# Decode attention over a paged cache: keys transposed by VectorE in 32x32 blocks, scores as 32-row products in sixteen array tiles, in place of TensorE transposes

## The chip, the cores and the metric

The kernel runs on one core of one Trainium2 chip. The metric is the device time in microseconds (us) of one launch; smaller is better. Three timed executions of the kernel before are given, and one profiled execution, whose trace all rows below come from.

## What is computed

One inference step of a two-layer decoder trunk for 512 prompt tokens and 8 decode rows (one new token in each). Layer 0 is a state-space layer, layer 1 multi-head latent attention with 16 heads; each layer stands between two SwiGLU blocks. The change touches only the latent attention of the 8 decode rows over their 2048 cached positions:

```python
def latent_attention(q_lat, q_pe, q_pos, key_sets):
    for c, kpe, k_pos in key_sets:       # c (b,k,256), kpe (b,k,32)
        s = einsum('bqhr,bkr->bhqk', q_lat, c) + einsum('bqhe,bke->bhqk', q_pe, kpe)
        scores.append(where(k_pos <= q_pos, s * scale, NEG_BIG))
    p = softmax(concatenate(scores, -1), -1)
    return sum(einsum('bhqk,bkr->bqhr', p_part, c))
...
c_past = cache_ckv[page_table].reshape(b_s, 2048, 256)
kpe_past = cache_kpe[page_table].reshape(b_s, 2048, 32)
```

So for each decode row b: 16 pages of 128 positions, each page 128x256 latents and 128x32 rotary keys, 16 heads. Everything is float32.

## The kernel before

One program, an instruction stream for each engine written out by hand, with semaphores between them; no scheduler reorders anything. The big matrix products of the trunk (feed-forward, projections) fill most of the time; then come the attention of the prompt (eight pairs of heads, `for i in range(NH // 2)`, scores, softmax, transposed probabilities, weighted values), and behind it the decode rows, `for b in range(NB)`, and the output projection (`wo_half`, `product`), which begins inside the last decode row.

**The decode rows.** The pages of row b land in `cb[b % 3]` (latents, positions on partitions) and `kb[b % 3]` (rotary keys). `page_loader` issues them, SP (SyncE) pages 0 to 8 and POOL (GpSimd) pages 9 to 15, in the order pages 0, keys 0, pages 1, keys 1, keys 2, pages 2, keys 3, pages 3, keys 4 and so on; `pages(b)` waits until the row three before has been read by its last product (`d_o`), `pages(2)` until the prompt attention's last output is in place (`a_ol`). Behind `caches()` SP loads `uv` and the columns of the output projection.

A score needs the latent dimension on partitions, so the keys of a row are transposed on TensorE (PE): `turned(b, q)`, q = 0 to 8, four 128x128 transposes each into one PSUM bank (three banks in turn), 32 of latents and 4 of rotary keys. ScalarE (ACT) copies the even q to SBUF, VectorE (DVE) the odd ones, into `cbT` (and `kbT`). The scores of a row are then 8 products 128 rows x 32 columns x 512 positions with `qlat` and 16 of 128 positions with `qpe`, four at a time in the four column strips of the array, into one bank: partition 32c + h holds head h and the positions of pages 4c to 4c+3. DVE takes the maximum (L2291, L2292), ACT the exponential (L1532), PE transposes the probabilities (4 transposes), DVE copies them to SBUF as `pbT` (L2301), and PE makes the 16 weighted products with `cb` (L3258), which ACT copies to `ob` (L1537).

PE's order in iteration b of `for b in range(NB)`: scores of b, the turns 0 to 3 of row b+1, the transposes of the probabilities, turns 4 to 8 of row b+1, weighted products of b. So the turns fill the time of the softmax. The turns of row 0 stand between the last steps of the prompt attention. Row 7 has `wo_half` in their place.

```python
src = cb[j][:, 4 * (q % 4) + s, (q // 4) * P:(q // 4) * P + P]          # PE, turned
got = turn(ps[:, (0, 1, 7)[n % 3], s * P:s * P + P], src)
...
mm(ps[HP * c:HP * c + HP, 2 + j, :], qlat[:, r, b, :], cbT[:, r, KB * c:KB * c + KB], ...)   # PE, scores
```

Of the kernel before, what the change touches and what calls it, by code (L numbers as in the profile page):

```python
# [19 lines left out]
F32 = mybir.dt.float32  # L20
# [3 lines left out]
ALU = mybir.AluOpType  # L24
# [3 lines left out]
P = 128  # L28
# [42 lines left out]
KB = PAST // NQ  # L71
NEG = -1e30
# [184 lines left out]
def yoco_step(nc, inp, out):  # L257
# [6 lines left out]
    with ctx:  # L264
# [57 lines left out]
        with ExitStack() as s:  # L322
# [16 lines left out]
            with ExitStack() as m:  # L339
# [3 lines left out]
                    m, ("cbT", [P, RT, PAST], F32), ("cb2", [P, NPG, R], F32), ("mb", [P, NB], F32), ("nmb", [P, NB], F32),  # L343
# [82 lines left out]
        def pair_of(dst, s):  # L426
# [9 lines left out]
        kbT = tb[:, 0, 0:4 * P].rearrange("p (g k) -> p g k", g=4)  # L436
# [34 lines left out]
        d_uv, d_pt, d_t, d_ta, d_td, d_s, d_m, d_e, d_pt2, d_pe, d_o, d_oe, d_rt, d_w, d_we, d_ws, d_wp, d_l, d_fin, d_of, d_oh, d_ol = (  # L471
            sem("dec_" + n) for n in ("uv", "pt", "tr", "tr_a", "tr_d", "s", "max", "exp", "p_tr", "p_sb", "o", "o_sb", "rows",
                                      "logw", "w", "w_norm", "w_ps", "lat_ps", "fin", "of", "oh", "ol"))
        d_le = sem("dec_lat_rows")
# [146 lines left out]
        def page_loader(eng, arrived, ckv, kpe):  # L621
# [351 lines left out]
        def _(act):  # L973
# [508 lines left out]
            def turned(b, q):  # L1482

                act.wait_ge(d_t, b * 9 + q + 1)
                if b >= 1:
                    act.wait_ge(d_s, b)
                src = ps[:, (0, 1, 7)[(b * 9 + q) % 3], :]
                if q < 8:
                    run(cbT[:, q // 4, (q % 4) * 512:(q % 4) * 512 + 512], src, ACT.Copy).then_inc(d_ta, 1)
                else:  # L1490
                    run(kbT[:, :, :], src.rearrange("p (g k) -> p g k", g=4), ACT.Copy).then_inc(d_ta, 1)

            for i in range(NH // 2):
# [13 lines left out]
                if more:  # L1507
                    softmax(i + 1, 2)
                    softmax(i + 1, 3)
                else:  # L1510
                    turned(0, 0)
                probs(i, 4)
            turned(0, 2)
            turned(0, 4)
            weighted(NH // 2 - 1)
            turned(0, 6)
            turned(0, 8)


            for b in range(NB):  # L1520
                if b + 1 < NB:
                    turned(b + 1, 0)
                else:
# [8 lines left out]
                run(pb, ps[:, 2 + b % 2, :], ACT.Exp, bias=nmb[:, b:b + 1], scale=SCALE, accum_out=lb[:, b:b + 1]).then_inc(d_e, 1)  # L1532
                if b + 1 < NB:
# [3 lines left out]
                run(ob[:, b, :], ps[:, 5 + b % 2, 0:R], ACT.Copy).then_inc(d_oe, 1)  # L1537
# [1954 lines left out]
```

## Time and profile before

| | us |
|---|---|
| three timed executions | 2007.0, 2008.1 (median), 2010.79 |
| profiled execution, span from first to last instruction | 2007.1 |
| PE (matmul records) busy | 1960.4 (98% of the span) |
| PE weight loads busy | 1875.2 (93%) |
| DVE, ACT, POOL busy | 1277.0, 820.4, 132.8 |
| decode rows, from the first score to the last (1507.77 to 1578.34) | 70.6 |

The profile gives no total of its own for the profiled execution beside its span, which lies 1.0 us below the median of the timed ones. One float32 product is recorded as two weight loads and two matmuls (passes), one transpose as one of each, so a count behind an x is twice the number of float32 products. A bracket behind a row is the time that the engine was idle before it and what it waited for. "PEclk" is the granted TensorE clock as a share of 2.4 GHz.

### The profile page before, as it was taken

How to read it: one execution, taken by the hardware profiler on the slowest of the kernel's cores; microseconds unless marked ns; L12 is line 12 of the kernel's file. 1: busy time of each engine (PE TensorE's matmuls, PEld its weight loads, DVE VectorE, ACT ScalarE, POOL GpSimd, SP SyncE). 2: the span in 40 equal slices, each digit the busy share in tenths (PEclk: the TensorE clock that was granted, in tenths of full speed). 3: DMA queues.
4: the chain of work that ended last, by engine and by line, in shares of the span. 5: the costliest groups of instructions: out<-in, count | busy, mean ns of one | idle time of the engine just before them, and what ended most of it. 6: DMA issues, size and time to landing. Idle time of an engine off the chain costs nothing.

```text
span 2007.1 us, 41612 instructions
## 1 busy us (share of the span) xinstructions
PE 1960.4 (98%) x17604; PEld 1875.2 (93%) x17604; DVE 1277.0 (64%) x1771; ACT 820.4 (41%) x1243; POOL 132.8 (7%) x231
## 2 busy tenths in 40 slices
PE   8999999988999999999999999999989999999999
PEld 7999999987999999999999999997666799999998
DVE  6445486697469577576884856655764349668474
ACT  5332233343245244255452534454654244345252
POOL 3002002010000000000000000000047000000000
PEclk9999999989999999999999999999999999999999
DMA  7233234864342322234322322231248422323222
GB/s 151 84 102 88 75 93 115 269 140 100 95 137 85 120 89 95 77 105 116 97 85 85 127 85 86 84 101 51 54 119 231 149 71 83 127 85 120 91 74 75
DMA packets 260624, 211.55 MB, mean 105 GB/s; under 512 B 42372, under 2 KB 235426, under 8 KB 260450
## 3 DMA queue, kind: packets, MB, share of 16 engines
q1 hardware_dynamic: 248528, 187.52, 31.9%
q0 software_dynamic: 6656, 13.69, 2.4%
q10 hardware_dynamic: 5266, 7.85, 1.2%
q8 instruction: 130, 2.13, 0.4%
q14 instruction: 44, 0.36, 0.1%
HBM read 195.29 MB, written 10.33 MB: 102 GB/s over the span
## 4 chain that ended last, share of the span: by engine, by line
PE 67%; DVE 3%; ACT 2%; issue 2%; SPq 1%; DMA 1%; DVEq 0%; ACTq 0%
PE ps L2459 25%; PE ps L2487 25%; PE ps L2388 6%; PE ps L2401 2%; PE ps L2947 1%; PE ps L3053 1%; PE ps L3209 1%; PE ps L3086 1%; SPq L654 1%; SPq L639 1%; DMA cb<-cache_ckv 1%; PE ps L2841 1%; PE ps L3030 1%; DVE wl L1668 0%; DVE xl L1619 0%
## 5 line engine op out<-in xcount | busy, mean ns | idle before, releaser
L2388 PE MATMUL ps<-xh,wh 128*128 128x260 f32 x1088 | 286.9, 285 | 2.6 <-DVE xl L1619 1.4
L2388 PE MATMUL ps<-xl,wh 128*128 128x260 f32 x1088 | 283.7, 283 | 0.0
L2487 PE MATMUL ps<-xoh,wh 128*128 128x260 f32 x992 | 281.3, 284 | 1.3 <-DVE sq L1835 1.3
L2487 PE MATMUL ps<-xoh,wl 128*128 128x260 f32 x992 | 281.0, 283 | 0.0
L2487 PE MATMUL ps<-xol,wh 128*128 128x260 f32 x992 | 280.6, 283 | 0.0
L2459 PE MATMUL ps<-xh,wh 128*128 128x260 f32 x872 | 228.8, 284 | 0.6 <-DVE wl L1668 0.6
L1067 ACT ACTIVATE wh<-rw 128x1024 fp32r<-128x1024 f32 (+1 forms) x135 | 138.8, 1029 | 218.6 <-PE ps L2459 151.7
L2459 PE MATMUL ps<-xl,wh 128*128 128x260 f32 x872 | 227.0, 282 | 0.0
L2388 PE MATMUL ps<-xh,wl 128*128 128x260 f32 x1088 | 219.3, 283 | 0.0
L990 ACT ACTIVATE wh<-raw 128x1024 fp32r<-128x1024 f32 (+1 forms) x90 | 100.4, 1116 | 283.4 <-PE ps L2388 250.5
L2388 PEld LDWEIGHTS ps<-xh,wh 128*128 128x128 f32 x1088 | 205.6, 189 | 6.9 <-issue 3.9
L2388 PEld LDWEIGHTS ps<-xl,wh 128*128 128x128 f32 x1088 | 205.1, 188 | 0.0
L1668 DVE TENSOR_TENSOR wl<-rw,wh 128x1024 fp32r<-128x1024 f32 (+1 forms) x135 | 160.3, 1188 | 67.3 <-ACT wh L1067 67.2
L2487 PE MATMUL ps<-xoh,third 128*128 128x260 f32 x1040 | 198.6, 283 | 0.6 <-DVE sq L1835 0.6
L2487 PEld LDWEIGHTS ps<-xoh,wh 128*128 128x128 f32 x992 | 186.6, 188 | 1.6 <-DVE wl L1668 1.6
L2487 PEld LDWEIGHTS ps<-xol,wh 128*128 128x128 f32 x992 | 186.9, 188 | 0.0
L2487 PEld LDWEIGHTS ps<-xoh,wl 128*128 128x128 f32 x992 | 186.8, 188 | 0.0
L1579 DVE TENSOR_TENSOR wl<-raw,wh 128x1024 fp32r<-128x1024 f32 (+1 forms) x92 | 120.5, 1310 | 89.5 <-ACT wh L990 81.8
L2459 PE MATMUL ps<-xh,wl 128*128 128x260 f32 x872 | 175.5, 283 | 0.0
L2388 PEld LDWEIGHTS ps<-xh,wl 128*128 128x128 f32 x1088 | 167.9, 189 | 0.0
L2459 PEld LDWEIGHTS ps<-xh,wh 128*128 128x128 f32 x872 | 164.4, 189 | 1.7 <-DVE wl L1668 1.1
L2487 PEld LDWEIGHTS ps<-xoh,third 128*128 128x128 f32 x1040 | 164.8, 188 | 0.8 <-DVE third L1668 0.8
(550 smaller groups left out, 4202.2 us busy)
## 6 DMA issues: line engine op xcount, KB each, us to landing
rw<-ffn_w_gate SPq DMA_DIRECT2D x33, 1024.0 KB, 5.4
rw<-ffn_w_up SPq DMA_DIRECT2D x33, 1024.0 KB, 8.0
rw<-ffn_w_down SPq DMA_DIRECT2D x12, 2048.0 KB, 7.8
raw<-ffn_w_gate SPq DMA_DIRECT2D x22, 512.0 KB, 3.9
raw<-ffn_w_up SPq DMA_DIRECT2D x22, 512.0 KB, 3.9
raw<-ffn_w_down SPq DMA_DIRECT2D x16, 704.0 KB, 4.8
rw<-ffn_w_down SPq DMA_DIRECT2D x6, 1536.0 KB, 6.7
cb<-cache_ckv SPq DMA_DIRECT2D x72, 128.0 KB, 3.7
```

The source lines that it names most:

```text
L639: eng.dma_start(kb[j][:, g, :], inp["cache_kpe"][bass.ds(numbers[b][g], 1)].rearrange("a p r -> p (a r)")).then_inc(arrived[j], 16)
L654: eng.dma_start(cb[j][:, g, :], inp["cache_ckv"][bass.ds(numbers[b][g], 1)].rearrange("a p r -> p (a r)")).then_inc(arrived[j], 16)
L990: run(wh[par_][:, 0:size], raw[par_][:, 0:size], ACT.Copy).then_inc(w_hi, 1)
L1067: run(as_slot(name, slot_h(name, n), n), raw_of(name, n), ACT.Copy).then_inc(z_hi, 1)
L1579: tt(wl[par_][:, 0:size], raw[par_][:, 0:size], wh[par_][:, 0:size], ALU.subtract).then_inc(w_lo, 1)
L1668: tt(as_slot(name, slot_l(name, n), n), raw_of(name, n), as_slot(name, slot_h(name, n), n), ALU.subtract).then_inc(z_lo, 1)
L2388: got = mm(ps[0:width, bank + half, 0:HALF], w[par_][:, k * width:k * width + width], src[:, k0 + k, half * HALF:half * HALF + HALF], star ...
L2401: return nc.tensor.transpose(dst, src, ident[0:rows, 0:rows])
L2459: got = mm(ps[:, bank + half, T0], w[:, cols], src_[:, k, half * HALF:half * HALF + HALF], start=first and m == 0 and s == 0, stop=last an ...
L2487: got = mm(ps[:, bank + mat, T0], w[:, cols], src[:, j, k, :], start=first and k == 0 and m == 0 and s == 0, stop=k == 3 and m == 1, skip_ ...
L2841: got = mm(ps[:, bank + half, 0:HALF], w[slot][:, k * P:k * P + P], src[:, k, half * HALF:half * HALF + HALF], start=k == 0 and m == 0 and ...
L2947: got = mm(ps[:, 2 * (i % 2) + half, 0:HALF], cols, src[:, k, half * HALF:half * HALF + HALF], start=k == 0 and o == 0 and s == 0, stop=k ...
```

## The change

1. **Keys.** `turned` goes from PE, ACT and DVE to DVE alone: five `V.transpose` instructions a row, each of which transposes every 32x32 block where it stands, SBUF to SBUF: q = 0 the rotary keys (128x512), q = 1 to 4 a quarter of the latents each (64 of 256 columns of all 16 pages, 128x1024). Partition group g (32 partitions) of `cbT` then holds latent dimension within a block of 32, for the positions 32g to 32g+31 of each page.
2. **Scores.** A product now contracts over 32 rows only: `cache_scores(b, q)`. For each of 8 blocks of 32 latent dimensions, and once for the rotary keys, 16 products of 32 rows x 16 heads (32 columns for the rotary keys) x 128 positions, one for each of the four row groups g and four column strips c: 144 products a row in place of 24. Row group g adds up in bank `SC_BANK + g`, so the scores of a row take four banks, 128 columns each, and there is one set of them.
3. **Queries.** Since each row group multiplies all 256 latent dimensions, `qlat` is copied to all four partition groups (`qrep`, in the columns of `cst` that held the cosines): 16 DMAs of 32 partitions x 256 elements on POOL's queue, ahead of its `caches()`.
4. **Softmax.** DVE's maximum and ACT's exponential read the four banks; ACT instead of DVE copies the transposed probabilities.
5. **Waits.** The exponential of row b must have read the banks before the scores of row b+1 begin. `keys(b)` waits for turn 0 of the row three before, not for all nine turns.

```diff
@@ the scores' views, page_loader
-        kbT = tb[:, 0, 0:4 * P].rearrange("p (g k) -> p g k", g=4)
+        kbT = tb[:, 0, 0:NPG * DR].rearrange("p (g e) -> p g e", g=NPG)
+        qrep = cst[:, C_COS:C_COS + NRB * NB * NH].rearrange("p (q r b h) -> p q r b h", q=NQ, r=RT, b=NB)
+        sc = ps[:, SC_BANK:SC_BANK + NQ, 0:P]
...
-                    eng.wait_ge(d_t, 9 * (b - 2))
+                    eng.wait_ge(d_t, TURNS * (b - 3) + 1)
@@ ACT, for b in range(NB)
-                run(pb, ps[:, 2 + b % 2, :], ACT.Exp, bias=nmb[:, b:b + 1], scale=SCALE, accum_out=lb[:, b:b + 1]).then_inc(d_e, 1)
-                if b + 1 < NB:
-                    for q in range(2, 9, 2):
-                        turned(b + 1, q)
+                run(pb.rearrange("p (s g t) -> p g s t", s=NQ, g=NQ), sc.rearrange("p g (s t) -> p g s t", s=NQ), ACT.Exp,
+                    bias=nmb[:, b:b + 1], scale=SCALE, accum_out=lb[:, b:b + 1]).then_inc(d_e, 1)
+                act.wait_ge(d_pt2, b + 1)
+                if b >= 1:
+                    act.wait_ge(d_o, b)
+                run(pbT[:, :, :], ps[:, PT_BANK, :].rearrange("p (m q) -> p m q", m=NQ), ACT.Copy).then_inc(d_pe, 1)
@@ DVE, turned(b, q)
-                dve.wait_ge(d_t, b * 9 + q + 1)
-                if b >= 1:
+                j = b % 3
+                if q == 0:
+                    dve.wait_ge(d_in[j], (b // 3 + 1) * 16 * N_SP)
+                    dve.wait_ge(d_kin[j], (b // 3 + 1) * 16 * N_POOL)
+                    if b == 0:
+                        dve.wait_ge(a_s, NH // 2 * NSS)
+                if b >= 1 and q < NTP:
+                    dve.wait_ge(d_sp, NTP * (b - 1) + q + 1)
+                elif b >= 1:
                     dve.wait_ge(d_s, b)
-                copy(cbT[:, q // 4, (q % 4) * 512:(q % 4) * 512 + 512], ps[:, (0, 1, 7)[(b * 9 + q) % 3], :]).then_inc(d_td, 1)
+                if q == 0:
+                    V.transpose(kbT, kb[j][:, :, :]).then_inc(d_t, 1)
+                else:
+                    cols = slice(RG * TURN_W * (q - 1), RG * TURN_W * q)
+                    V.transpose(cbT[:, :, cols], cb[j][:, :, cols]).then_inc(d_t, 1)
@@ DVE, for b in range(NB)
+                if b + 1 < NB:
+                    turned(b + 1, 0)
                 dve.wait_ge(d_s, b + 1)
-                own(V.tensor_reduce(mb[:, b:b + 1], ps[:, 2 + b % 2, :], AX.X, ALU.max))
+                own(V.tensor_reduce(mb[:, b:b + 1], sc, AX.XY, ALU.max))
                 ts(nmb[:, b:b + 1], mb[:, b:b + 1], -SCALE, None, ALU.mult).then_inc(d_m, 1)
                 if b + 1 < NB:
-                    turned(b + 1, 1)
-                    turned(b + 1, 3)
+                    for q in range(1, TURNS):
+                        turned(b + 1, q)
@@ PE
+            def cache_scores(b, q):
+
+                pe.wait_ge(d_t, TURNS * b + q + 1)
+                if q == 0 and b == 0:
+                    pe.wait_ge(d_qr, 16 * NQ * NQ)
+                    pe.wait_ge(a_ol, NH // 2)
+                elif q == 0:
+                    pe.wait_ge(d_e, b)
+                for k in range(TURN_W * (q - 1), TURN_W * q) if q else (NRB,):
+                    for g in range(NQ):
+                        rows = slice(RG * g, RG * (g + 1))
+                        for c in range(NQ):
+                            pages_ = slice(NQ * c, NQ * (c + 1))
+                            if k < NRB:
+                                heads, w, src = NH, qrep[rows, k % NQ, k // NQ, b, :], cbT[rows, pages_, RG * k:RG * (k + 1)]
+                            else:
+                                heads, w, src = HP, qpe[rows, b, g, :], kbT[rows, pages_, :]
+                            got = mm(ps[HP * c:HP * c + heads, SC_BANK + g, 0:P], w, src, start=q == 0, stop=k == NRB - 1, skip_group_check=True)
+                got.then_inc(d_sp if q < NTP else d_s, 1)
...
                 for m in range(NQ):
-                    got = turn(ps[:, 4, m * P:m * P + P], pb[:, m * P:m * P + P])
+                    got = turn(ps[:, PT_BANK, m * P:m * P + P], pb[:, m * P:m * P + P])
                 got.then_inc(d_pt2, 1)
                 if b + 1 < NB:
-                    for q in range(4, 9):
-                        turned(b + 1, q)
+                    cache_scores(b + 1, 0)
...
+                weighted_rows(b)
+                if b + 1 < NB:
+                    for q in range(1, TURNS):
+                        cache_scores(b + 1, q)
@@ POOL, ahead of caches()
+            pool.wait_ge(l_qe, 1)
+            for g in range(NQ):
+                for k in range(NQ):
+                    pool.dma_start(qrep[RG * g:RG * (g + 1), k, :, :, :], qlat[RG * k:RG * (k + 1), :, :, 0:NH]).then_inc(d_qr, 16)
```

**PE, from the last transposes of the prompt attention's probabilities (`pp`) to the weighted products of row 0.** First before, then now. `cb` and `kb` are transposed keys, `pT,vv` the last pair's values, `ta` the probabilities of the decode rows; an x counts instructions.

```order
L2401 MATMUL ps<-cst,pp 128x128 x3
L2401 MATMUL ps<-cst,cb 128x128 x16
L3086 MATMUL ps<-pT,vv 64x512 x2
...
L2401 MATMUL ps<-cst,kb 128x128 x4
L3223 MATMUL ps<-cbT,qlat 32x512 x8
L3227 MATMUL ps<-tb,qpe 32x128 x16
L2401 MATMUL ps<-cst,cb 128x128 x16
L2401 MATMUL ps<-cst,ta 128x128 x4
L2401 MATMUL ps<-cst,cb 128x128 x16
L2401 MATMUL ps<-cst,kb 128x128 x4
L3258 MATMUL ps<-cb,ta 32x256 x16
```

```order
L2398 MATMUL ps<-cst,pp 128x128 x20
L3083 MATMUL ps<-pT,vv 64x512 x2
...
L3203 MATMUL ps<-tb,qpe 32x128 x16
L3203 MATMUL ps<-cbT,cst 16x128 x128
L2398 MATMUL ps<-cst,ta 128x128 x4
L3203 MATMUL ps<-tb,qpe 32x128 x16
L3213 MATMUL ps<-cb,ta 32x256 x16
```

No key transposes are left on PE: between the probabilities' transposes and the weighted products stand only the 16 rotary products of the next row, and its 128 latent products follow behind.

**DVE, the loop over decode rows, from the weighted output (`xl`) of the prompt's last pair through row 1's maximum.** First before, then now; `tb` holds the transposed rotary keys, `mb` and `nmb` the maximum, `ta` the copied probabilities.

```order
L2235 TENSOR_TENSOR xl<-ps,xh 128x512
L2247 COPY cbT<-ps 128x512
L2291 TENSOR_REDUCE mb<-ps 128x1
L2292 TENSOR_SCALAR nmb<-mb 128x1
L2247 COPY cbT<-ps 128x512 x2
L2301 COPY ta<-ps 128x512
L2247 COPY cbT<-ps 128x512 x2
L2291 TENSOR_REDUCE mb<-ps 128x1
```

```order
L2226 TENSOR_TENSOR xl<-ps,xh 128x512
L2249 STREAM_TRANSPOSE cbT<-cb 128x16x64 x3
L2246 STREAM_TRANSPOSE tb<-kb 128x512
L2295 TENSOR_REDUCE mb<-ps 128x1
L2296 TENSOR_SCALAR nmb<-mb 128x1
L2249 STREAM_TRANSPOSE cbT<-cb 128x16x64 x4
L2246 STREAM_TRANSPOSE tb<-be 128x512
L2295 TENSOR_REDUCE mb<-ps 128x1
```

The rotary transpose of the next row, which waits until that row's pages have landed, now stands ahead of the maximum of the present row.

## Rows read from the trace of the kernel before

**Rows 1.** The page's head.

```profile
span 2007.1 us, 41612 instructions
```

**Rows 2.** Timeline of PE in the decode rows: start, us, instruction, [idle before].

```profile
1529.80 2.00 PE L2401 MATMUL ps<-cst,cb 128*128 128x128 f32 x16 [0.49 <-DMA cb<-cache_ckv]
1531.81 0.66 PE L2401 MATMUL ps<-cst,ta 128*128 128x128 f32 x4
1532.30 1.94 PE L2401 MATMUL ps<-cst,cb 128*128 128x128 f32 x16
...
1534.71 1.93 PE L3258 MATMUL ps<-cb,ta 128*32 128x256 f32 x32
1536.46 1.90 PE L3223 MATMUL ps<-cbT,qlat 128*32 128x512 f32 x16
...
1539.16 2.00 PE L2401 MATMUL ps<-cst,cb 128*128 128x128 f32 x16
...
1568.97 2.00 PE L2401 MATMUL ps<-cst,cb 128*128 128x128 f32 x16 [0.95 <-DMA cb<-cache_ckv]
...
1578.34 0.39 PE L3209 MATMUL ps<-xh,wh 128*128 128x260 f32 x1
```

**Rows 3.** Timeline of SP's queue: when it issues the pages and keys.

```profile
1507.16 4.45 SPq L654 DMA_DIRECT2D cb<-cache_ckv  x9
...
1553.88 4.56 SPq L639 DMA_DIRECT2D kb<-cache_kpe  x8
1558.62 4.83 SPq L654 DMA_DIRECT2D cb<-cache_ckv  x9
```

**Rows 4.** Windows: us, busy PE, PEld, DVE, ACT, POOL, PEclk, DMA share, GB/s.

```profile
1507.77:1578.34 70.57, 68.41 (x889) 47.87 (x889) 30.86 (x51) 29.39 (x58) 43.98 (x82) 1.00 0.79 229
```

**Rows 5.** Groups of DVE by form in the whole span: busy, mean ns, idle before.

```profile
L1680 DVE TENSOR_TENSOR be<-rw 128x1024 f32<-128x1024 f32 x15 | 18.3, 1218 | 0.0
...
L2086 DVE TENSOR_TENSOR x<-x,tb 128x512 f32<-128x512 f32 x8 | 8.9, 1114 | 0.0
...
L2291 DVE TENSOR_REDUCE mb<-ps 128x1 f32<-128x512 f32 x8 | 5.5, 691 | 32.4 <-PE ps L3227 32.4
...
L2292 DVE TENSOR_SCALAR nmb<-mb 128x1 f32<-128x1 f32 x8 | 1.2, 154 | 0.3
```

**Rows 6.** Timeline of PE in the state-space layer: products in fewer and smaller tiles.

```profile
443.72 1.89 PE L2853 MATMUL ps<-sn,ct 128*32 128x8 f32 x128 [0.81 <-ACT last_in L1302]
...
470.30 1.97 PE L2804 MATMUL ps<-tsh,ush 128*64 128x128 f32 x32 [0.18 <-ACT yr L1313]
472.19 1.98 PE L2817 MATMUL ps<-ctcw,xsr 64*64 64x128 f32 x64
```

**Rows 7.** Groups of ACT by form in the decode rows, 1507 to 1580.

```profile
L1489 ACT ACTIVATE cbT<-ps 128x512 f32<-128x512 f32 x28 | 16.7, 597 | 29.1 <-PE ps L2401 29.1
L1532 ACT ACTIVATE ta<-ps,nmb 128x512 f32<-128x512 f32 x8 | 5.5, 682 | 1.2 <-DVE nmb L2292 1.2
...
L1532 ACT ACTIVATION_READ_ACCUMULATOR ta<-ps,nmb 128x1 f32 x8 | 1.6, 200 | 0.0
```

**Rows 8.** Timeline of PE at the end of the prompt attention.

```profile
1501.37 1.94 PE L2401 MATMUL ps<-cst,cb 128*128 128x128 f32 x16
1503.25 2.37 PE L3086 MATMUL ps<-pT,vv 128*64 128x512 f32 x16
```

**Rows 9.** Windows, columns as in rows 4: PE idle, then the granted clock.

```profile
475.20:477.00 1.80, 0.00 (x0) 0.00 (x0) 1.73 (x5) 1.80 (x4) 0.00 (x0) 1.00 0.00 0
477.05:478.96 1.91, 1.91 (x65) 1.74 (x65) 1.87 (x2) 0.32 (x1) 1.64 (x4) 1.00 0.00 0
...
1484.70:1488.00 3.30, 1.46 (x12) 1.02 (x10) 3.06 (x7) 1.48 (x5) 2.83 (x6) 1.00 1.05 311
1488.10:1491.40 3.30, 3.15 (x15) 2.69 (x16) 1.27 (x5) 1.41 (x5) 3.14 (x7) 0.50 0.66 91
```

**Rows 10.** Timeline of POOL: its first decode pages.

```profile
1466.20 4.05 POOL L654 DMA_DIRECT2D cb<-cache_ckv  x7 [150.32 <-DMA qs<-qq]
```

More of the change, by code:

```diff
@@ L71 @@
 KB = PAST // NQ
+RG = P // NQ
+NRB = R // RG
+TURN_W = 2
+NTP = NRB // TURN_W
+TURNS = NTP + 1
+SC_BANK, PT_BANK = 4, 3
 NEG = -1e30
@@ L2269, in _ @@
                 else:
-                    turned(0, 1)
+                    turned(0, 0)
                 probs(i, 5)
@@ L2277, in _ @@
                     normalise(i + 1, 3)
-            turned(0, 3)
-            turned(0, 5)
+            turned(0, 1)
             weighted(NH // 2 - 1)
-            turned(0, 7)
+            for q in range(2, TURNS):
+                turned(0, q)
             def wide_lo(j):
@@ L3185, in _ @@
                 turned_probs(i, 3)
-                if not more:
-                    turned(0, 0)
                 turned_probs(i, 4)
-                if not more:
-                    turned(0, 1)
                 turned_probs(i, 5)
@@ L3193, in _ @@
                     values(i // 2 + 1, i % 2)
-            for q in range(2, 6):
-                turned(0, q)
             weighted(NH // 2 - 1)
-            for q in range(6, 9):
-                turned(0, q)
             def wo_half(d, half, k0, k1):
@@ new lines, in weighted_rows @@
+            def weighted_rows(b):
+                pe.wait_ge(d_pe, b + 1)
+                if b >= 2:
+                    pe.wait_ge(d_oe, b - 1)
+                for m in range(NQ):
+                    for c in range(NQ):
+                        got = mm(ps[HP * c:HP * c + HP, 1 + b % 2, 0:R], pbT[:, m, HP * c:HP * c + HP], cb[b % 3][:, 4 * c + m, :],
+                                 start=m == 0, stop=m == NQ - 1, skip_group_check=True)
+                got.then_inc(d_o, 1)
+            for q in range(TURNS):
+                cache_scores(0, q)
@@ L3234, in _ @@
+            for b in range(NB):
                 if b == NB - 1:
-                    pe.wait_ge(a_ol, NH // 2)
                     wo_half(0, 0, 0, KD)
@@ L3248, in _ @@
                     turn(ps[0:NB, 7, P:2 * P], lb[:, :]).then_inc(d_rt, 1)
+                    pe.wait_ge(d_oe, NB - 1)
                     wo_half(1, 0, 0, 3)
-                pe.wait_ge(d_pe, b + 1)
-                if b >= 2:
-                    pe.wait_ge(d_oe, b - 1)
-                elif b == 1:
-                    pe.wait_ge(a_ol, NH // 2)
-                for m in range(NQ):
-                    for c in range(NQ):
-                        got = mm(ps[HP * c:HP * c + HP, 5 + j, 0:R], pbT[:, m, HP * c:HP * c + HP], cb[b % 3][:, 4 * c + m, :],
-                                 start=m == 0, stop=m == NQ - 1, skip_group_check=True)
-                got.then_inc(d_o, 1)
+                weighted_rows(b)
+                if b + 1 < NB:
+                    for q in range(1, TURNS):
+                        cache_scores(b + 1, q)
             wo_half(1, 0, 3, KD)
+            pe.wait_ge(d_oe, NB)
             wo_half(2, 0, 0, 3)
```

68 lines of the change are left out of this document (6 added, 62 removed).

## The prediction

> **What bounds the kernel now.** Look at the windows first. In the 70.6 us of the decode rows PE is busy for 68.4, at a granted clock of 1.00 (2.4 GHz), DVE for 30.9 and ACT for 29.4 [rows 4]. PE looks like the bound, and the timeline of PE says what a decode row costs it, by the starts of the rows: 1529.80 to 1539.16 is 9.36 us, of which 1.75 are the weighted products (1534.71 to 1536.46), 0.49 the transposes of the probabilities (1531.81 to 1532.30), 2.70 the scores (1536.46 to 1539.16), and the rest, 4.42, the transposes of the keys [rows 2]. The same timeline shows a second bound close behind: PE waits for a page DMA at 1529.80 and again at 1568.97, in front of rows 3 and 7. These two are four rows apart, 39.17 us, so pages arrive every 9.79 us, just slower than PE's 9.36. SP's queue says why. Eight issues of keys and nine of pages follow each other without a wait: keys at 1553.88, pages at 1558.62, done at 1563.45, so 9.57 us for one row's issues [rows 3]. The last pages land 10.35 us after SP began to issue them (1558.62 to 1568.97), and 9.37 us later the last score is done and `wo_half` begins at 1578.34 [rows 2, 3].
>
> So the change has to be read against the page traffic. It takes work from PE, but the pages set the pace of rows 3 to 7, and the change moves none of their DMAs. What it can win is the start of the chain and what lies behind the last landing.
>
> **PE's part.** Removed: 4.42 us of transposes a row and 2.70 of scores. Added: 144 products, 288 records by the trace's count. What one costs is the question. The nearest rows: 64 records of 64x64 tiles (four tiles, two row groups) with 128 columns take 1.98 us, 30.9 ns each, while 32 records of 128x64 tiles with the same columns take 1.97, 61.6 ns each [rows 6]. Halving the rows of a tile halved the time of a record: row groups do run beside each other. Sixteen tiles are four times as many as four, so I take 30.9/4 = 7.7 ns: 288 x 7.7 = 2.2 us a row. The bounds: at the cheap end nothing below that, since the columns must stream; at the dear end 30.9 ns (four tiles at once only), 8.9 us a row. Between them lies the row of 128 records with 8 columns, 1.89 us, 14.8 ns each [rows 6], which carries weight loads of twice the columns and mostly no streaming, so issue alone costs at most that.
>
> The Trainium skill has a rule that speaks against the change: in "TensorE: Matmul & The Clock Gate", section "Wait — 56ns, not 53.3ns?", start-to-start never drops below about 25 ns, however small the product. By that rule the change loses; it is the first rival below. The trace does not bear it out: 14.8 ns is already less.
>
> **DVE's part.** Removed: four copies and the copy of the probabilities a row. Added: one transpose of 512 elements and four of 1024 a partition. No row shows a DVE transpose. The nearest is an SBUF to SBUF operation of 128x1024 float32, 1.22 us [rows 5]; at the same rate 512 take some 0.69, as the reduction of 512 does. I take these: 0.69 + 4 x 1.22 = 5.6 us, plus 0.69 for the maximum and 0.15 for the scaling, 6.4 a row with nothing waiting. The dear end is the strided addition of 512 elements at 1.11 us, 2.2 ns an element: 2.2 us for 1024, 10 for a row's transposes [rows 5].
>
> **ACT's part.** It loses five copies and gains the copy of the probabilities, 0.60, after its exponential of 0.68 and 0.20 for the sum [rows 7]; half its load is gone, so it costs nothing but its place in the chain.
>
> **The cycle.** With one set of score banks PE can't score ahead any more. From the last score of a row: maximum and scaling 0.84, exponential and sum 0.88, transposes of the probabilities 0.49, weighted products 1.75, and four handovers and their latencies, which I put at 0.7 (an estimate): 4.7 us, plus 288 records. At 7.7 ns the copy of the probabilities isn't covered by the 32 rotary records and adds about 0.4: 7.3 us. DVE's own cycle is 6.4 and some 0.4 of handovers. Both are below 9.79, so the pages stay the bound. The cycle meets 9.79 at (9.79 - 4.7)/288 = 17.7 ns a record. Below that PE's price hardly counts, above it every ns costs 0.29 us a row.
>
> **The order of DVE.** Turn 0 of row b+1 stands ahead of the maximum of row b and waits for row b+1's pages. So row b's softmax is held until those have landed, and with it `d_o`, which frees the buffer for row b+3: landing, about 5.9 us to the end of the weighted products (the first six terms below, with their handovers), then 10.35 to land again, 16.3 for two rows, 8.1 a row. Below 9.79, so it doesn't slow the queue. But it moves row 6's softmax behind the last landing: from there, rotary turn 0.69, maximum 0.84, exponential 0.88, transposes 0.49, copy 0.60, weighted 1.75, the 256 latent records 2.0 and handovers 0.5: 7.7 us (DVE's side, 0.69 + 0.84 + 4.9 + 0.6, is 7.0). Before it was 9.37. Gain 1.7.
>
> **The start.** PE loses 16 transposes between the last probabilities and the last weighted product, 1501.37 to 1503.25 [rows 8]; DVE gets the rotary turn of 0.69 ahead of the copy that product waits for. I take 1.0 of the 1.9 as won; `a_ol` and with it SP's pages of row 2 (1507.16) come that much sooner, and the whole chain of pages with them. The query copies lie in the 150 us in which POOL waits for nothing else [rows 10]: hidden, and if the cover were gone, 16 of POOL's issues at 0.58 (4.05/7 by the same row), 9 us, would stand ahead of the pages.
>
> **The clock.** PE will be idle for about 5 us of every 9.8, where before it had no gap over a microsecond. An idle stretch may cost it the full clock: in 1484.70 to 1488.00 it was busy for 1.46 of 3.30, and the next 3.30 us ran at 0.50 (1.2 GHz); after 1.80 us of idleness at 475.20 it ran on at 1.00 [rows 9]. At half clock the last chain grows by 0.5 + 1.75 + up to 1.8 = 4.0 us. I charge 0.7: which of the products fall into a slow stretch is open, and a part of the loss hides under DVE's side of the tail, which has 0.7 us to spare.
>
> **Sum** against the profiled span, 2007.1 [rows 1]: -1.0 - 1.7 + 0.7 = -2.0, so 2005.1; on the median, 1.0 above it, 2006.1 us. Runs of this kernel scatter by about 0.2%, 4 us, so this would read as no change.
>
> **Rivals.**
> *Products cost more than 17.7 ns* (ends slower). For: 31 ns in four tiles, and no row has sixteen; against: the halving from 61.6 to 30.9, and 14.8 ns. At 25 ns the cycle is 4.7 + 7.2 = 11.9, and row 0's scores end 7.2 us after 1506.2: 1513.4 + 7 x 11.9 = 1596.7, 18.4 later than 1578.34: 2026.5. At 30.9: 13.6 a cycle, 1515.1 + 95.2 = 1610.3: 2040. The rule of the skill would give the first of these. Chance 0.18.
> *DVE transposes at the strided price.* DVE's cycle is 1.1 + 4 x 2.25 + 0.84 + 0.4 = 11.3: 1506.2 + 3 x 2.25 + 0.6 + 7 x 11.3 = 1592.7, +14.3: 2022.4. Against: the blocks read runs of 64 elements. Chance 0.10.
> *The clock falls in every row.* The tail's 4.0 instead of 0.7, and as much of `wo_half` at half clock: +1.3 to +4 in all, 2009.4 to 2012. At 14.8 ns a record some 2 more. Chance 0.12.
> *The pages come faster.* An undisturbed issue of SP takes 4.45/9 = 0.49 us [rows 3], 17 of them and the gaps between the groups 8.8; if PE's lighter load lets the queue run at that pace, five rows win 0.8 each on top of 2.7: 2001. Against: both queues and the DMA engines see the same traffic. Chance 0.10.
> *Row groups take turns*, so that the change doesn't do what it says: 27 to 31 ns, part of the first rival.
> The forecast has 0.50.
>
> **How the numbers follow.** Slower by over 0.2%: the first two rivals, 0.28, half of the third's worst, 0.04, and 0.02 of the forecast: 0.34. Faster: most of the fourth, 0.09, and 0.06 of the forecast, whose start may win the whole 1.9. Within: 0.51. The range goes from 2001.0 to 2024.0: it takes in DVE's rival and the clock's, and leaves out the dear products.
>
> **What would show it.** PE's timeline: groups of 128 `cbT` products, some 1 us for 128 records; above 2.3 (17.7 ns) the first rival holds. DVE's groups: transposes of 128x1024 at 1.22. PE waiting for DVE's turn 0 and that for the DMA, rows 9.8 us apart. PEclk in the windows of 1510 to 1580. If the rows come at under 9 us apart, or the last score is later than 1580, I am wrong.

## The result, and the profile after

| | before | changed |
|---|---|---|
| four timed executions each, median (lowest to highest), us | 2007.95 (2007.0 to 2010.79) | 2036.15 (2035.85 to 2036.27) |
| ratio, 95% interval | | 1.0124 (1.0106 to 1.0143) |
| span of the profiled execution, us | 2007.1 | 2034.3 |
| last decode score done, us | 1578.34 | 1604.10 |

The change costs 28 us, and 26 of them are there when the last score is done. The forecast of 2006.1 was wrong, and its range, up to 2024, did not hold the time. This is the timeline of PE in the changed kernel over two rows, with the columns of [rows 2]; L3203 is `cache_scores` (`tb`: rotary, `cbT`: latent), L3213 `weighted_rows`, L2398 `turn`.

```profile
1527.42 0.65 PE L2398 MATMUL ps<-cst,ta 128*128 128x128 f32 x4 [1.79 <-ACT ta L1521]
1528.37 0.51 PE L3203 MATMUL ps<-tb,qpe 32*32 32x128 f32 x32 [0.29 <-issue]
1528.81 1.94 PE L3213 MATMUL ps<-cb,ta 128*32 128x256 f32 x32
1530.68 1.04 PE L3203 MATMUL ps<-cbT,cst 32*16 32x128 f32 x64
1532.94 1.85 PE L3203 MATMUL ps<-cbT,cst 32*16 32x128 f32 x128 [1.23 <-issue]
1537.24 1.47 PE L3203 MATMUL ps<-cbT,cst 32*16 32x128 f32 x64 [2.46 <-issue]
1540.50 1.11 PE L2398 MATMUL ps<-cst,ta 128*128 128x128 f32 x4 [1.78 <-ACT ta L1521]
1541.54 0.73 PE L3203 MATMUL ps<-tb,qpe 32*32 32x128 f32 x32
1542.30 3.64 PE L3213 MATMUL ps<-cb,ta 128*32 128x256 f32 x32
1545.87 3.69 PE L3203 MATMUL ps<-cbT,cst 32*16 32x128 f32 x250
1551.85 0.40 PE L3203 MATMUL ps<-cbT,cst 32*16 32x128 f32 x6 [2.29 <-issue]
1554.04 1.11 PE L2398 MATMUL ps<-cst,ta 128*128 128x128 f32 x4 [1.79 <-ACT ta L1521]
```

The two rows start 13.08 and 13.54 us apart, where before it was 9.36 and the pages' pace 9.79 [rows 2]. (Over six rows, from 1516.43 to 1592.66, the mean is 12.7.) The second one, read against the forecast's cycle of 7.3 us, term by term: the transposes of the probabilities take 1.04 instead of 0.49, the rotary products 0.76 where 0.25 was charged for them (32 records at 7.7 ns) and 0.4 for the copy that outlasts them, the weighted products 3.57 instead of 1.75, the latent products 3.69 and 0.40 instead of 2.0, an idle stretch of 2.29 that no term had, and 1.79 of waiting for the exponential, which holds the 1.72 forecast for maximum, exponential and sum.

The windows, with the columns of [rows 4], say why some of these are twice what they should be (PEclk is the last column but two): the whole stretch of decode rows; the stretch of 10.2 us in which the clock stayed down; and 128 latent records at full clock.

```profile
1508.00:1604.00 96.00, 67.32 (x2556) 40.87 (x2556) 46.22 (x55) 14.21 (x30) 44.13 (x82) 0.77 0.59 170
```

```profile
1536.46:1546.66 10.20, 7.61 (x176) 3.81 (x185) 5.97 (x7) 1.76 (x4) 3.81 (x8) 0.50 0.56 158
```

```profile
1532.94:1534.79 1.85, 1.85 (x128) 1.41 (x128) 0.18 (x1) 0.00 (x0) 1.67 (x5) 1.00 0.92 218
```

The mean granted clock of the decode rows fell from 1.00 [rows 4] to 0.77: the transposes, rotary and weighted products of most rows run at 0.50 (1.2 GHz). The latent products are dear for another reason: 128 records take 1.85 us, 14.5 ns each, at the full clock.

What was idle, from the waits of 1508 to 1604 (who waited for whom, us in total, times, longest):

```profile
ACT ta L1521 <- DVE nmb L2296: 47.2, 7, 8.5
DVE mb L2295 <- PE ps L3203: 41.4, 7, 7.5
...
PE ps L3203 <- issue: 15.3, 9, 2.5
POOL cb L662 <- PE ps L3213: 15.2, 3, 5.8
...
PE ps L2398 <- ACT ta L1521: 12.6, 7, 1.8
...
DVE tb L2246 <- DMA cb<-cache_ckv: 0.4, 1, 0.4
```

DVE waits for PE's scores and practically never for pages (0.4 us), while POOL waits for PE before it may load the next row. The bound has moved from the pages to PE, which is itself idle: 12.6 us for the exponentials and 15.3 us for nothing that the profile shows. DVE is as forecast, in its groups (columns as in [rows 5]):

```profile
L2249 DVE STREAM_TRANSPOSE cbT<-cb 128x1024 f32<-128x1024 f32 x32 | 37.0, 1212 | 0.0
L2295 DVE TENSOR_REDUCE mb<-ps 128x1 f32<-128x512 f32 x8 | 5.5, 692 | 49.4 <-PE ps L3203 49.4
```

The idle stretches have a companion in the DMA queues of 1508 to 1604 (packets, MB, share of 16 engines). This is the changed kernel:

```profile
q8 instruction: 19, 0.31, 1.4%
```

And the kernel before, in the same stretch:

```profile
q8 instruction: 9, 0.15, 0.6%
```

A packet has 16 KB (0.31 MB / 19). Each record of PE stands for a weight load and a matmul, so 128 records are 256 instructions, and if a packet holds those it has 64 bytes for each. The Trainium skill, "Perfetto Trace Analysis", section "The 4-stage abstract model", calls instructions 64-byte ones, which gives the same. Theory SUPPLY: these packets are PE's own instruction stream, and PE runs dry when short products use up a block faster than the next one comes.

The totals of whole executions bear out whose packets they are. The kernel before, with 17604 records of PE, the changed kernel, with 19236, and the kernel of experiment 10 with three row groups, with 20796, read:

```profile
q8 instruction: 130, 2.13, 0.4%
```

```profile
q8 instruction: 143, 2.34, 0.5%
```

```profile
q8 instruction: 155, 2.54, 0.5%
```

1632 records more are 12.75 blocks of 128, and 13 packets more; 1560 more are 12.2 blocks, and 12 packets.

### The profile page after: what moved, and what is told of

Read it like the earlier page. It is cut to its first block, busy times and chain, and to the rows that moved or that the text cites. A ratio compares the mean times of both kernels' runs of the same rounds, so it can differ in the third digit from the quotient of the medians.

```text
span 2034.3 us, 44797 instructions
## 1 busy us (share of the span) xinstructions
PE 1963.4 (97%) x19236; PEld 1870.8 (92%) x19236; DVE 1291.5 (63%) x1771; ACT 803.1 (39%) x1211; POOL 143.1 (7%) x247
## 4 chain that ended last, share of the span: by engine, by line
PE 68%; DVE 4%; issue 3%; ACT 2%; DVEq 0%; ACTq 0%
PE ps L2456 25%; PE ps L2484 24%; PE ps L2385 6%; PE ps L3203 2%; PE ps L2398 2%; PE ps L3213 1%; PE ps L2944 1%; PE ps L3050 1%; PE ps L3181 1%; PE ps L3083 1%; PE ps L3027 1%; PE ps L2838 1%; DVE wl L1659 0%; DVE xl L1610 0%; DVE mx L2201 0%
```

## The experiments

Times of all but the two bursts are medians of at least four executions, each ratio against the kernel before on the same chip. On those chips the executions scattered by up to 13 us, so a difference of a few us between two of them is not a finding; the profiles carry the argument.

**1. Keep the clock up: wide products in the gap.**

```diff
+            def filler(b, n):
+                if b < NB - 1:
+                    for _ in range(n):
+                        mm(ps[:, 0, :], ident, cb[b % 3][:, 0:2, :].rearrange("p g r -> p (g r)"), start=True, stop=True, ...)
...
+            filler(0, 2)
...
                     for q in range(1, TURNS):
                         cache_scores(b + 1, q)
+                    filler(b + 1, 2)
```

> Added: behind the last score of rows 0 to 6 TensorE issues two float32 products 128x128 by 512 columns into a bank that nothing reads (an estimate of 0.9 to 1.8 us, in the 1.8 us in which it waits for the exponential). Theory CLOCK (the rows are long because TensorE runs at 1.2 GHz in their first half): the granted clock in 1508 to 1604 rises from about .75 to over .9, the weighted products of a row take 1.94 us instead of 3.64 and the row pace falls from 12.8 to about 11: 2036 - 7 x 1.8 = 2023 us. Theory SUPPLY (TensorE's instruction stream is fetched in blocks and runs dry once or twice a row under the dense short products): the idle stretches put down to issue (15.3 us, 9 times in 96 us) stay, so no more is won than the clock's part, and what the faster clock wins is partly taken by longer stretches of that kind: 2026 to 2034. Theory RECORDS (a product simply costs 14 ns a record at any clock): no change of the latent products' time, 2028.

Measured: 2035.28 us, ratio 1.0124 (1.0091 to 1.0157). The timeline of PE over one row and a half:

```profile
1544.04 1.06 PE L2398 MATMUL ps<-cst,ta 128*128 128x128 f32 x4
1545.03 0.51 PE L3203 MATMUL ps<-tb,qpe 32*32 32x128 f32 x32
1545.79 1.93 PE L3219 MATMUL ps<-cb,ta 128*32 128x256 f32 x32 [0.25 <-ACT ta L1526]
1547.65 1.70 PE L3203 MATMUL ps<-cbT,cst 32*16 32x128 f32 x110
1549.69 1.87 PE L3203 MATMUL ps<-cbT,cst 32*16 32x128 f32 x128 [0.34 <-issue]
1553.44 0.45 PE L3203 MATMUL ps<-cbT,cst 32*16 32x128 f32 x18 [1.88 <-issue]
1553.81 1.98 PE L3210 MATMUL ps<-cb,cst 128*128 128x512 f32 x4
```

The weighted products are at 1.93 us in every row, and the time did not move. It lies above what any of the three theories gave: the stretches of issue grew to 17.7 us (L3203 and L3210 together), among them one of 4.61, and the filler itself took 2 to 3.8 us. So the half clock alone does not explain the loss. The rows are 13.05 us apart in the mean (1518.33 to 1596.61, six rows). They show two more things. Where two stretches follow each other within a row's scores, exactly 128 records lie between them, as in the changed kernel at 1532.94. And a stretch that in the changed kernel stood behind record 250 of its row stands here behind record 110 + 128 = 238, 12 earlier. By then three fillers of four records each have been added. The same holds row by row: 201 (0 added), 192 against 184 (8), 250 against 238 (12), 181 against 165 (16), 239 against 219 (20), 170 against 146 (24) and 228 against 200 (28). PE stops at fixed places of its instruction stream, whatever it waits for in the program.

**2. One wide product instead of two** (`filler(b + 1, 1)`).

> One wide product behind the last score of rows 0 to 6 instead of two; at full clock the two took 1.98 us, so one takes 1.0, inside the 1.79 us of waiting. Theory CLOCK ADDS (half clock costs a row 2.4 us: 1.7 in the weighted products, 0.45 and 0.23 in the transposes and rotary products): if one product keeps the clock, 2036 - 7 x 2.4 = 2019; the earlier run with two showed the full clock and lost as much in front of the transposes. Theory NOT ENOUGH: one product does not keep the clock in most rows, weighted products of 3.6 us stay and the time with them: 2034 to 2038. Theory SUPPLY says that the stretches of issue stay in either case (12 to 16 us in 1508 to 1604), their places in the stream two records a row earlier than in the changed kernel.

Measured: 2028.95 us, ratio 1.0094 (1.0057 to 1.013). Mean clock 0.86 instead of 0.77, weighted products 385 ns in the mean instead of 548, rows 11.9 us apart (1517.31 to 1576.89, five rows). The stretches of issue grew to 19.2 us, 11 times. One of 4.37 us, 1583.09 to 1587.46, lies beside the large loads of the output projection, in a window with the DMA share at 1.08. So the time came down by some 7 us of the 28, which the intervals of the two ratios, overlapping as they do, leave uncertain by several; the theory that only the clock costs time had asked for 17. The clock was won in a part only, and the longer stretches are time that came back as waiting for instructions. The clock also changes the price of the latent products, which the changed kernel's rows show less clearly: 98 records from 1587.46 took 2.04 us at 0.50, 20.8 ns each, and 125 from 1524.04 2.61 us, 20.9 ns.

**3. Fewer products.** Half, then three quarters of the latent blocks:

```diff
-                for k in range(TURN_W * (q - 1), TURN_W * q) if q else (NRB,):
+                for k in ((q - 1) * TURN_W,) if q else (NRB,):
```

> Left out: every second block of latent scores, so 80 products (160 records) a row instead of 144 (288); VectorE's transposes all stay. Theory SUPPLY: 128 instructions and their weight loads less a row, the stretches of issue fall from 15.3 us to under 5, the row pace from 12.8 to about 9.8 to 10.5 where the pages bound it again: about 2008 to 2014 us. Theory RECORDS: 128 records x 14 ns = 1.8 us a row off, 12.8 to 11.0: 2024 us, the stretches of issue as before. Theory CLOCK: TensorE does less, so the clock stays low or falls further; 2024 or later.

> Left out: two of the eight blocks of latent scores, so 112 products (224 records) a row. Theory SUPPLY (a block of the stream is 128 records; 261 records a row instead of 325): one stretch of issue less in three rows besides the 0.95 us of the records themselves, stretches 5 to 9 us in all, total 2018 to 2024. Theory RECORDS: 64 x 14.8 ns = 0.95 us a row, 7.6 in all: 2028.

Measured: half, 2011.11 us, ratio 1.0003 (0.9992 to 1.0014); three quarters, 2020.5, ratio 1.0054 (1.0034 to 1.0073). With half the blocks, the waits of 1508 to 1581 read:

```profile
DVE tb L2246 <- DMA cb<-cache_ckv: 22.2, 6, 5.1
...
PE ps L3203 <- issue: 2.2, 1, 2.2
```

Now DVE waits for pages in front of six rows, as the forecast had it for the whole change, and the only stretch of issue is 2.2 us. The weighted products still take 3.5 to 3.6 us in five of seven rows: the half clock is there and costs the rows little, since the pages pace them (experiment 4 tests that). By the record (14.5 ns) the missing products are worth 64 x 14.5 = 0.93 us a row for each quarter, 7.4 us in all. The first quarter won some 15 us (15.7 by the medians, 14 by the ratios), and its stretches of issue fell from 15.3 us to 10.3 (5 to 9 were expected; the time lies in the expected 2018 to 2024).

**4. Half of the blocks and one wide product** (the edits of 2 and 3 together).

> Left out: every second block of latent scores (80 products a row); added: one wide product behind the last score of rows 0 to 6. Without the addition this kernel took as long as the kernel before, with the weighted products at 3.6 us in six of seven rows and VectorE waiting 22 us for pages. Theory PAGES BOUND IT: the full clock shortens work that is hidden behind the pages, 2008 to 2011, with weighted products at 1.94 us if the product keeps the clock. Theory CLOCK: the half clock is still on the path, 2.4 us a row off: 1995 to 2003.

Measured: 2011.75 us, ratio 1.0009 (0.9999 to 1.0019), weighted products at 505 ns in the mean instead of the 548 of experiment 3, and DVE waiting 23.4 us for pages. The clock was won in three of seven rows (1.93 us for the weighted products), and behind those rows PE waited some 5 us for the exponential, which the next pages held up, where behind the others it waited some 1. So it did not move the time: with few instructions the pages are the bound.

**5. Less page traffic.**

```diff
+                rows = slice(0, P if b < 3 else 16)
                 for g in ckv:
-                    eng.dma_start(cb[j][:, g, :], ...)
+                    eng.dma_start(cb[j][rows, g, :], ...[rows])
```

> Left out: for rows 3 to 7 only 16 of 128 positions of each latent page are loaded (an eighth of the page traffic, the same number of DMAs). Theory SUPPLY with contention (the instruction blocks of 16 KB are late because the pages hold the DMA engines): the stretches of issue vanish in the rows whose time no longer has page traffic, the row pace falls to about 11 there: 2036 - 5 x 2 = 2026. Theory SUPPLY by density alone: the blocks take as long, stretches and time stay: 2034 to 2037. Theory CLOCK or RECORDS: no change, 2034 to 2037. Theory PAGES (the traffic is the bound as forecast): 2015 or less.

Measured: 2032.98 us (2025.54 to 2034.48), ratio 1.0114 (1.0091 to 1.0138). The stretches stand behind the same records (250, 181, 239, 170, 228), from 1.27 to 1.96 us long in place of 1.56 to 2.29. Together they are 7.7 us in place of 9.6; three are shorter, one is the same and one longer (1.96 in place of 1.56). So the traffic may lengthen them, and it is not what makes them; most of the loss is there without it: the time lies between the 2026 expected of contention and the 2034 to 2037 of density alone, nearer to the latter. The profiled execution is the fastest of the four, the one of 2025.54 us.

**6. The order of DVE:** `turned(b + 1, 0)` behind the maximum.

> VectorE takes turn 0 of row b+1 (the rotary keys, 0.69 us) behind the maximum of row b instead of ahead of it, so the softmax of row b no longer waits for the pages of row b+1. My forecast charged that order with nothing because the pages set the pace; since the pages do not bound the rows now, turn 0 is done long before the last score and every theory expects no change: 2035 to 2037. If the row b+1 pages still held the softmax, up to 0.7 us a row would be won: 2031.

Measured: 2033.89 us, ratio 1.0113 (1.0084 to 1.0143). No change, as expected.

**7. Another order on PE:** long products among the short ones.

```diff
-                weighted_rows(b)
...
+                    cache_scores(b + 1, 1)
+                    weighted_rows(b, 0, 2)
+                    cache_scores(b + 1, 2)
+                    weighted_rows(b, 2, NQ)
+                    cache_scores(b + 1, 3)
+                    cache_scores(b + 1, 4)
```

> The same instructions in another order on TensorE: scores 1 of row b+1 ahead of the weighted products of b, scores 2 between their halves, scores 3 and 4 behind. Theory SUPPLY: the stretches of issue come from blocks of 128 short records in a row; with 32 long records (60 to 114 ns each) spread among them the block lasts longer than its fetch and the stretches fall from 15 us to some 8: 2028, and the copy of the probabilities is covered. Theory DENSITY OVER A ROW (325 records a row are too many in any order): 2034 to 2038. Theory RECORDS or CLOCK: 2034 to 2038, since neither changes; a change of the tile form costs something, up to 0.2 us a row.

Measured: 2036.54 us, ratio 1.0126 (1.0101 to 1.0151). The stretches fell to 10.7 us, and the rows did not come faster (1540.67, 1553.75, 1567.58), most of them with the weighted products at half clock still (514 ns in the mean). The 2028 of theory SUPPLY was missed: shorter stretches did not bring shorter rows. I don't have every us of this run; it shows that spreading the short products did not pay.

**8. Another order of the tiles:** by diagonals, `c = (g + o) % NQ`.

> The sixteen products of a block in another order: each differs from the one before in row group and column strip (by the diagonal), where the changed kernel runs four strips of one row group. Theory ISSUE (14.8 ns is the rate at which TensorE takes a weight load and a matmul, whatever tile they go to): 128 records stay at 1.85 to 1.88 us, 2034 to 2038. Theory TILES (row groups run beside each other, strips of one row group do not): 128 records fall towards 1.0 us, 1.7 us a row less, and the stretches of issue grow by a part of that: 2024 to 2032.

Measured: 2033.68 us, ratio 1.013 (1.0097 to 1.0163). 128 records take 1.85 us as before: between these two orders the price does not depend on which tile follows which.

**9. Short products in the kernel before,** 64 a row, of one row group, ahead of its scores:

```diff
+                for n in range(64):
+                    c = n % NQ
+                    mm(ps[HP * c:HP * c + HP, 2 + j, 0:P], qlat[0:HP, n // NQ % RT, b, :], cbT[0:HP, 0, P * c:P * c + P], ...)
```

> The kernel before, with 64 products (128 records) of 32x32 tiles with 128 columns ahead of the scores of each row, whose result the scores overwrite. TensorE's 9.36 us a row become 11.3, above the pages' 9.79, so 8 rows cost at least 8 x 1.9 - 3 = 12 us: 2019 to 2022 if 128 short records are worth 1.9 us and no more (theory RECORDS). Theory SUPPLY: 270 records a row in all, of which half are long, so a block of 128 lasts 4 us on the mean; stretches of issue in some rows only, 0 to 6 us more: 2020 to 2027. That the stretches occur in the old order of work too, where VectorE does no transposes, would show that they do not belong to the change's waits.

Measured: 2050.01 us, ratio 1.019 (1.0158 to 1.0222), far more than either theory gave. The timeline of PE over a row:

```profile
1539.21 1.93 PE L3262 MATMUL ps<-cb,ta 128*32 128x256 f32 x32
1541.07 3.70 PE L3223 MATMUL ps<-cbT,qlat 32*32 32x128 f32 x128
1544.70 3.62 PE L3227 MATMUL ps<-cbT,qlat 128*32 128x512 f32 x16
1548.08 1.11 PE L3231 MATMUL ps<-tb,qpe 128*32 128x128 f32 x32
```

Windows of the two middle groups:

```profile
1541.07:1544.77 3.70, 3.70 (x136) 3.50 (x136) 0.00 (x0) 0.38 (x1) 2.73 (x6) 1.00 0.63 186
1544.77:1548.00 3.23, 3.23 (x16) 0.74 (x20) 0.00 (x0) 0.00 (x0) 2.99 (x6) 0.50 0.97 306
```

On one row group 128 records take 3.70 us at the full clock, 28.9 ns each, twice the price on four. And behind them the clock is at 0.50, the scores 3.62 us instead of 1.92, although PE had no idle stretch at all from 1520 to 1620. So it is in five of the seven rows of this stretch; in the other two (1555.90 and 1600.25) the scores behind the short products take 1.92. So short products on 32-row tiles can be followed by the half clock where nothing waits. The rows come 14.8 us apart (1524.68 to 1613.38, six rows) in place of 9.36: 3.6 of the 5.4 are the added products, and the rest is mostly the half clock, which neither theory had charged. There are no stretches of issue here, against what SUPPLY had expected for some rows: 128 records in 3.70 us are about as slow as the pieces of experiment 10 (3.5 to 3.75 us), and long products follow them.

**10. Bursts** in the changed kernel, two executions each: behind row 2 and row 6, 256 products on two row groups; then, behind six wide ones, 384 on three.

```diff
...
+                for i in range(n):
+                    g, c = i // NQ % 3, i % NQ
+                    rows, bank = slice(RG * g, RG * (g + 1)), (0, 3, 1 + b % 2)[g]
+                    mm(ps[HP * c:HP * c + NH, bank, 0:P], qrep[rows, c, 0, b, :], cb[b % 3][rows, c, 0:P], ...)
...
+                        filler(b + 1, 6)
+                        burst(b + 1, 384)
```

> Added: 256 products (512 records) of 32x16 tiles with 128 columns, back to back and waiting for nothing, behind the last score of row 2 (page traffic beside them) and of row 6 (the large weight loads beside them), into banks that nothing reads. Theory SUPPLY: each burst breaks up into pieces of 128 records of 1.9 us with stretches of issue between them, 1.3 us or more each and longer where the DMA engines are busy: 11 to 18 us a burst, 2058 to 2072 us in all. Theory WAITS (the stretches belong to something that the scores of a row wait for, the transposes or the banks): the bursts run through, 7.6 us each: 2051.

> Added behind the last score of rows 2 and 6: six wide products (128x128 by 512 columns, about 6 us at full clock), then 384 products (768 records) of 32x16 tiles on three row groups in turn. The question is how fast blocks of 128 short records can come at all. In the runs so far a block of 1.9 us was followed by 1.88 us of idleness where nothing else disturbed it, 3.75 us a block; the burst on two row groups ran at half clock with 3.77 us a block and without gaps, so it could not tell the array's pace from the supply's. Three row groups need at most 2.5 us a block (29.4 x 2/3 = 19.6 ns a record at half clock), 1.9 at full clock. Theory SUPPLY WITH A FLOOR: pieces of 128 records, 3.75 us from start to start at either place, longer under page traffic: bursts of 22 us or more. Theory CONTENTION ONLY: with the DMA engines idle (behind row 6's large loads) the pieces follow each other without a gap, 11 to 15 us a burst. On the clock: after six wide products it is 1.00, and it falls to 0.50 within the burst although TensorE never stops, if short tiles are what lets it fall; theory IDLENESS (only waiting lets it fall) says 1.00 throughout.

Measured: 2063.69 and 2084.35 us. On two row groups each burst has one gap at a block's end (3.01 and 3.28 us) and then runs without one at half clock, 448 records in 13.19 us, 29.4 ns each; the time lies in the range of theory SUPPLY, but the pieces that it expected did not appear, so this burst decides nothing. On three, the timeline of PE behind row 6:

```profile
1618.87 3.74 PE L3218 MATMUL ps<-cb,cst 32*16 32x128 f32 x274
1624.78 2.93 PE L3218 MATMUL ps<-cb,cst 32*16 32x128 f32 x128 [2.16 <-issue]
1628.53 2.93 PE L3218 MATMUL ps<-cb,cst 32*16 32x128 f32 x128 [0.83 <-issue]
1632.29 2.93 PE L3218 MATMUL ps<-cb,cst 32*16 32x128 f32 x128 [0.83 <-issue]
1636.05 2.57 PE L3218 MATMUL ps<-cb,cst 32*16 32x128 f32 x110 [0.83 <-issue]
```

And its windows:

```profile
1618.87:1622.61 3.74, 3.74 (x275) 3.31 (x274) 0.00 (x0) 0.00 (x0) 0.00 (x0) 1.00 0.02 4
1624.78:1638.55 13.77, 11.28 (x495) 8.57 (x495) 0.00 (x0) 0.00 (x0) 0.00 (x0) 0.50 0.02 5
```

These products wait for nothing, the DMA share is 0.02, and still a piece of 128 begins every 3.75 us (1624.78, 1628.53, 1632.29, 1636.05). Behind row 2 the same: 1547.17, 1550.92, 1554.68, then 3.48 and 3.47. The first 180 and 274 records run through, at 13.7 to 14.2 ns; I read this as what had been fetched while PE did long work. With it the bursts took 20.1 and 19.7 us, between the 22 or more of a floor from the first record and the 11 to 15 of contention alone. In the second burst, 1618.87 to 1638.55, five instruction packets moved, about one for each piece. That speaks for SUPPLY with a floor and against contention: about 3.5 to 3.75 us for 128 records, 27 to 29 ns a record, for as long as the stream is dense. What sets these 3.75 us no run shows.

On the clock the burst does not decide: it stayed at 1.00 through 3.74 us of short products and fell behind an idle stretch of 2.16. And a fourth row group brings nothing at the full clock: 13.7 ns a record on three here, 14.5 on four in the latent products.

## Why the prediction was wrong

**The bound: wrong for the change as it is.** The forecast had PE's cycle at 7.3 us, below the pages' 9.79, "so the pages stay the bound". It measured 12.7, and DVE waited for pages for 0.4 us in all. The order of the steps in the cycle was right, and so was the idea that pages hide a cycle that stays below them: with half the score products they pace the rows, PE's half clock is hidden, and the kernel takes as long as before.

**The step that failed: the cost of an added record, 7.7 ns.** I took the row of 1.98 us for 64 records [rows 6], divided 30.9 ns by four for sixteen tiles, and read the row of 128 records in 1.89 us [rows 6] as an upper bound on issue. It was near the price: 14.5 ns, at either tile order, with the clock at 1.00. Of the four-fold gain the row groups gave a two-fold one (28.9 ns on one group, 14.5 on four; the tiles on one group had 32 columns, those on four 16). That alone is 256 x 6.8 ns = 1.7 us a row and would still have been covered: 14.5 is below 17.7.

**What was missing: a price for the stream itself.** The sum had no term for how fast PE's instructions arrive. A dense stretch costs 29 ns a record once what was fetched ahead is used up, and the nearest row could not show that, since it was one block long (128 records). A row of 324 records is 2.53 blocks, 9.5 us at 3.75 a block. Spread evenly that would still be below the pages' 9.79; but the 256 latent records come in one run, which outpaces the supply once what was fetched ahead is used up, and PE's stops stand in a chain in which everything else waits for its scores. They show as the stretches of issue, 15.3 us over the eight rows, some 2 us a row. The first rival (products dearer than 17.7 ns) came nearest, with 2026.5 at 25 ns and 2040 at 30.9; that these lie on both sides of 2036 is luck, since its mechanism, the tiles, was wrong: a record costs 14.5 ns while the supply lasts, and the stops and the half clock make up the rest. The Trainium skill's floor of about 25 ns, "TensorE: Matmul & The Clock Gate", section "Wait — 56ns, not 53.3ns?", does not hold within a block here (14.5 ns), and is near what is sustained (29.3 ns, or 3.75 us for 128), which here comes from the supply.

**The clock: mis-sized, and its cause named only in part.** I charged 0.7 us in all and called a fall in every row a rival at 2009 to 2012. It fell in nearly every row: 1.7 us in the weighted products, 0.5 in the transposes, 0.3 in the rotary ones, 2.5 us a row. That rival priced the fall with the pages still pacing the rows; it is hidden only as long as they do. Idleness, the forecast's only cause, plays a part as far as experiment 1 shows, where wide products in the gap kept the full clock; but it is not needed: in experiment 9 the fall came behind 3.7 us of uninterrupted short products. What share each has in the changed kernel stays open.

**How the parts add up.** A row at half clock without a stretch, 1516.43 to 1527.42, took 10.99 us. The same at full clock would be 10.99 - 2.5 = 8.5, covered by the pages. With 2.3 us of stretches and full clock it would be 10.8, with both it is 13.3 (measured 13.1 to 13.5). The pages cover 9.79. So neither part alone explains 12.7 us a row: over seven rows, the half clock alone would cost (10.99 - 9.79) x 7 = 8 us, the stretches alone 7, and together they reach 25. This is an estimate, added up and not measured by itself. The runs of experiment 3 (-15.7, -25) fit it. Those of experiments 1 and 2 do in part: with their own stretches (2.6 and 2.3 us a row) and fillers the same parts give some 12.2 and 11.2 us a row, and 13.05 and 11.9 were measured; some 0.3 to 0.4 of the difference are latent products at the half clock, and about half a us a row stays open. Left over are about 1.4 us behind the last score (2034.3 - 1604.10 against 2007.1 - 1578.34), where the output projection starts at half clock.

**DVE: right,** 1.212 us and 0.67 where 1.22 and 0.69 were taken; the strided rival is out. **Its order: right,** worth nothing. **The query copies: right,** hidden. **The start:** SP's pages of row 2 left at 1506.31 with half the products, 0.85 us sooner than before, near the 1.0 forecast; in the changed kernel's profile they left at 1508.83, after an attention part with one more slow stretch, so this stays unsettled. **The tail:** with half the products 9.8 us from row 7's landing (1569.06) to the last score (1578.82), 2.1 more than forecast; its transposes and weighted products ran at half clock (1.12 and 3.64 us instead of 0.6 and 1.9).

No version of the change that I can see wins. Even with half of its products it takes as long as the kernel before, because the pages, close behind PE there, hold both. I didn't build one that keeps part of the transposes on PE.

## What to carry to other kernels

Count instructions as well as their time: when a change replaces few long products by many short ones, divide the longest dense stretch by what a block of the stream holds (128 float32 records here) and charge 3.75 us a block wherever the products take less; what was fetched ahead comes off that. Here a row's 256 latent records are two blocks, 7.5 us by this rule, and they took 6.0 in the mean, from 3.8 to 8.0, with their stops, where the forecast had 2.0. A row that prices one short burst does not price a stream of them. And before calling a slower clock hidden, name what hides it and how much slack it has once the other added costs are in.

## What the runs showed that I had not expected

- PE's instructions come in blocks, and PE stops at fixed places of the stream. The floor is 3.5 to 3.75 us for 128 short records and their loads, with the DMA share at 0.02; beside large loads a stretch reached 4.6 us.
- The profile gives such a stop as "issue", with nobody to release it; the instruction packets (19 against 9 in the same 96 us) are its only other trace that I found.
- 128 records of 32-row tiles take 3.70 us on one row group and 1.85 on four, both at the full clock.
- Behind 3.7 us of such products the granted clock fell to 0.50 without any idleness in five of seven rows (experiment 9), and through 13 us of them on two row groups, with no gap, it stayed there (experiment 10).
